# Decoder step on one core: a shared weight unit for the index columns, rotary by shuffles, array halves in turn, 25 tiles a chunk step

## What is computed

```python
def _rope(x, pos):                       # the first quarter of each head is rotated
    x1, x2 = x[..., :half], x[..., half:rot]
    return jnp.concatenate([x1 * cos - x2 * sin, x2 * cos + x1 * sin, x[..., rot:]], axis=-1)
...
    proj = h @ p['w_in']
    qa, ka, va, qi, ki, wi, ga, gb = _split_last(proj[..., :N_IN_A], COLS_A)
    qa = _rope(qa...); ka = _rope(ka...)            # 8 heads of 128
    qi = _rope(qi...); ki = _rope(ki...)            # 8 index queries and 1 index key of 64
    o_a = attn_fn(qa, ka, va, qi, ki, wi)           # index scores pick the keys to attend to
    pb = proj[..., N_IN_A:]                         # r, k, v, decay 64, a 64, gate 160 columns
    o_b, wkv = _rwkv7(pb, pb_prev, wkv0, p)         # delta-rule state, token by token
    mixed = sigmoid(ga) * (o_a @ w_pa) + sigmoid(gb) * (o_b @ w_pb)
    x = x + mixed @ p['w_o']
    # then RMSNorm, SwiGLU, residual
```

## Time and profile before

| | us |
|---|---|
| median of 3 runs (lowest, highest) | 2019.15 (2017.89, 2021.63) |
| the profiled execution: first to last instruction (span) | 2018.5 |
| TensorE matmul busy | 1977.0 (98%) |
| VectorE busy | 1059.1 (52%) |
| ScalarE busy | 731.0 (36%) |

### The profile page before, as it was taken

The page is one execution under the profiler, slowest core; times in us unless marked ns, Lnnn a source line. Parts: engine busy times, 40 slices in busy tenths (PEclk is TensorE's granted clock), DMA queues, the critical chain, the costliest instruction groups (busy, mean ns, idle before and its releaser), DMA issues.

```text
span 2018.5 us, 38203 instructions
## 1 busy us (share of the span) xinstructions
PE 1977.0 (98%) x15709; PEld 1796.7 (89%) x15709; DVE 1059.1 (52%) x1265; ACT 731.0 (36%) x964; POOL 44.4 (2%) x63
## 2 busy tenths in 40 slices
PE   8999999999999999999999999999999999999996
PEld 7999776678875776699999999999999999999996
DVE  6655976378873520254445554444444445444434
ACT  6333101532233110244444454444444444333332
POOL 0000002200000000000000000000000000000000
PEclk9999998999999999999999999999999999999998
DMA  6544257344558899844456554444444444654543
GB/s 266 178 153 163 105 193 184 95 135 139 171 198 293 286 387 385 316 147 165 166 180 211 190 175 163 164 165 163 165 164 164 166 165 153 206 170 159 170 158 117
DMA packets 103625, 378.15 MB, mean 187 GB/s; under 512 B 26994, under 2 KB 36850, under 8 KB 76146
## 3 DMA queue, kind: packets, MB, share of 16 engines
q1 hardware_dynamic: 78802, 346.88, 49.2%
q0 software_dynamic: 4736, 18.80, 2.9%
q10 hardware_dynamic: 20000, 11.28, 2.0%
HBM read 359.30 MB, written 17.58 MB: 187 GB/s over the span
## 4 chain that ended last, share of the span: by engine, by line
PE 93%; DVE 3%; DMA 1%; SPq 1%; ACT 1%; issue 1%; DVEq 0%; ACTq 0%
PE ps L467 17%; PE ps L1080 14%; PE ps L1081 14%; PE ps L1082 14%; PE ps L1035 5%; PE ps L1036 5%; PE ps L1037 5%; PE ps L500 2%; PE ps L499 2%; PE ps L501 2%; PE ps L942 1%; PE ps L991 1%; PE ps L511 1%; PE ps L663 1%; DVE arena L1703 1%; DMA ring<-in_wst 1%
## 5 line engine op out<-in xcount | busy, mean ns | idle before, releaser
L2006 DVE TENSOR_TENSOR weights_lo<-ring,weights_hi 128x2048 fp32r<-128x2048 f32 (+1 forms) x152 | 305.6, 2011 | 284.8 <-ACT weights_hi L1523 284.8
L1081 PE MATMUL ps<-h_lo,weights_hi 128*128 128x288 f32 x1408 | 416.1, 296 | 0.0
L1080 PE MATMUL ps<-h_hi,weights_hi 128*128 128x288 f32 x1408 | 414.6, 294 | 0.3 <-DVE weights_lo L2006 0.3
L1082 PE MATMUL ps<-h_hi,weights_lo 128*128 128x288 f32 x1408 | 412.5, 293 | 0.0
L1523 ACT ACTIVATE weights_hi<-ring 128x2048 fp32r<-128x2048 f32 (+1 forms) x152 | 257.1, 1691 | 365.7 <-PE ps L1082 356.7
L467 PE MATMUL ps<-hT,ring 128*128 128x288 f32 x1472 | 384.9, 414 | 0.0
L467 PEld LDWEIGHTS ps<-hT,ring 128*128 128x128 f32 x1472 | 274.4, 191 | 79.5 <-issue 8.0
L1082 PEld LDWEIGHTS ps<-h_hi,weights_lo 128*128 128x128 f32 x1408 | 265.1, 188 | 0.0
L1080 PEld LDWEIGHTS ps<-h_hi,weights_hi 128*128 128x128 f32 x1408 | 264.2, 188 | 0.5 <-DVE weights_lo L2006 0.5
L1081 PEld LDWEIGHTS ps<-h_lo,weights_hi 128*128 128x128 f32 x1408 | 264.4, 188 | 0.1
L1080 PE MATMUL ps<-act_hi,weights_hi 128*128 128x288 f32 x704 | 208.4, 296 | 0.0
(11 more groups left out here) (356 smaller groups left out, 2953.5 us busy)
## 6 DMA issues: line engine op xcount, KB each, us to landing
ring<-in_wst SPq DMA_DIRECT2D x209, 1024.0 KB, 4.9
ring<-in_wdn SPq DMA_DIRECT2D x64, 704.0 KB, 4.1
arena<-in_v SPq DMA_DIRECT2D x64, 512.0 KB, 5.8
arena<-in_kT SPq DMA_DIRECT2D x112, 256.0 KB, 5.6
arena<-chunk_ar_bk ACTq DMA_DIRECT2D x24, 256.0 KB, 4.0
arena<-in_ki SPq DMA_DIRECT2D x64, 64.0 KB, 2.1
arena<-in_kT SPq DMA_DIRECT2D x8, 512.0 KB, 6.5
arena<-in_xT SPq DMA_DIRECT2D x4, 592.0 KB, 7.0
```

The lines of the kernel that those rows point to most:

```text
L1080: mm(out, W_HI[:, (u - U_FF) % 2, w], hi, start=start, stop=False)
L1081: mm(out, W_HI[:, (u - U_FF) % 2, w], lo, start=False, stop=False)
L1082: return mm(out, W_LO[:, u % 4, w], hi, start=False, stop=stop)
L2006: tt(W_LO[:, u % 4, 0:m], raw, W_HI[:, at, 0:m].bitcast(F32), ALU.subtract).then_inc(sem("w_split"), 1)
```

## The change

- **Shared unit.** The index key (64 columns) and index weights (8, padded to 32) move into the unit of the last 32 gate columns. The two units they filled are gone: 6 index units become 4. VectorE copies the rows out after unit 2 (two copies and a shuffle, 1633 to 1635 of the new file), and ScalarE's tanh and sigmoid wait for that. The gate's second product takes 128 rows of `G2` instead of 32.
- **Rotary by shuffles.** VectorE's `stream_shuffle` swaps rows inside groups of 32 partitions and the sign is in the sine table. The index rotary is four operations over all five blocks at once, after the gram masks; a chunk step's rotary is four operations on 32 partitions and two heads. All permutation matmuls are gone.
- **Halves in turn.** The lora products and the state terms alternate between the two halves of the array.
- **Tiles moved.** Six index tiles stand between the lora groups, the others follow the norm sums; a chunk step fills 25 tiles (4, 6, 5, 4, 6). One store buffer moves.

```diff
-U_SMALL, U_RKV, U_IDX, U_VKQ, U_GA, ... = 0, 3, 27, 33, 57, ...
+U_SMALL, U_RKV, U_IDX, U_VKQ, U_GA, ... = 0, 3, 27, 31, 55, ...
             for j in range(2 * CT):
+                if j % 4 == 0 and j:
+                    fill(U_IDX, j // 2 - 2, j // 2)
                 if j >= 4:
                     pe.wait_ge(sem("lora_out"), j - 3)
-                at = 64 * (j // CT)
-                mm(..., LORA[at:at + 64, (j % CT) * P:(j % CT + 1) * P], SW[at:at + 64, :],
+                at = 64 * (j % 2)
+                mm(..., LORA[at:at + 64, (j // 2) * P:(j // 2 + 1) * P], SW[at:at + 64, :],
...
-            tiles(U_IDX, U_VKQ, h_tok, NT)
+            fill(U_IDX, 6, 4 * KT)
+            vkq(-32, 0)
...
-            for j in range(5):
-                if j >= 2:
-                    fill(U_VKQ, 61 + 2 * j, 63 + 2 * j)
-                    pe.wait_ge(sem("rope_idx_out"), j - 1)
-                mm(ps[5 + j % 2][:, 0:NT], c_("ropeI"), IDXT[:, j, :], ...)
-            fill(U_VKQ, 71, 75)
-            pe.wait_ge(sem("rope_idx_out"), 5)
+            vkq(65, 75)
...
-                for at in (0, 64):
-                    for b in range(NB):
+                for b in range(NB):
+                    for at in (0, 64):
                         ins = mm(first[at:at + 64, j, :, b, :], SST[at:at + 64, j, b, :],
...
-                fill(U_VKQ, at, at + 5)
+                fill(U_VKQ, at, at + 4)
...
-                if n:
-                    rotate(2 * n - 2)
-                    rotate(2 * n - 1)
-                fill(U_VKQ, at + 18, at + 22)
+                fill(U_VKQ, at + 15, at + 19)
...
+                if u == 2:
+                    dve.wait_ge(sem("mixed"), 3)
+                    cp(KI[0:64], SG[0:64, 1, :]).then_inc(sem("index_rows"), 1)
+                    nc.vector.stream_shuffle(KI[64:P], SG[0:64, 1, :], list(range(32))).then_inc(...)
+                    cp(WI[64:64 + IH], SG[64:64 + IH, 1, :]).then_inc(sem("index_rows"), 1)
...
-            for j in range(5):
-                dve.wait_ge(sem("rope_idx"), j + 1)
-                x = IDXT[:, j, :]
-                ch(tt(ROPI[:, 0, :], ps[5 + j % 2][:, 0:NT], c_("sinI"), ALU.mult))
-                ch(tt(ROPI[:, 1, :], x, c_("cosI"), ALU.mult))
-                tt(x, ROPI[:, 0, :], ROPI[:, 1, :], ALU.add).then_inc(sem("rope_idx_out"), 1)
+            ch(nc.vector.stream_shuffle(flat(ROPI), flat(IDXT), swap_idx))
+            ch(tt(ROPI, ROPI, c_("sinI")..., ALU.mult))
+            ch(tt(IDXT, IDXT, c_("cosI")..., ALU.mult))
+            tt(IDXT, IDXT, ROPI, ALU.add).then_inc(sem("rope_idx_out"), 1)
...
             def rotate(n):
-                dve.wait_ge(sem("rope"), n + 1)
-                ...
+                dve.wait_ge(sem("bank_free"), U_VKQ + 2 + HA + 2 * n + 2)
+                x, t, shape = KQ[0:32, 2 * n:2 * n + 2, :], ROPT[0:32], [32, 2, NT]
+                ch(nc.vector.stream_shuffle(flat(t), flat(x), swap_head))
+                ch(tt(t, t, c_("sinA")[0:32]..., ALU.mult))
+                ch(tt(x, x, c_("cosA")[0:32]..., ALU.mult))
+                tt(x, x, t, ALU.add).then_inc(sem("rope_out"), 1)
```

More of the change, by code:

```diff
@@ L88, in constants @@
         sin[:half] = sin[half:rot] = np.sin(ang)
[L89 to L93, removed]
+        sin[:half] *= -1.0
         put("cos" + name, np.tile(cos, (reps, 1)))
@@ L364, in _ @@
             ki_pages(0)
-            units(8, U_VKQ + 7, unit)
+            units(8, U_VKQ + 9, unit)
             for c in range(NCH):
@@ L369, in _ @@
             ki_pages(1)
-            units(U_VKQ + 7, U_VKQ + 9, unit)
+            units(U_VKQ + 9, U_VKQ + 11, unit)
             ki_pages(2)
@@ L391, in k_half @@
                         "a p n -> p (a n)")[:, w]).then_inc(sem(f"k_in{half}"), 16)
-            units(U_VKQ + 9, U_GA + 1, unit)
+            units(U_VKQ + 11, U_GA + 1, unit)
             sp.wait_ge(sem("wkvs_out"), 16)
@@ L843, in chunk @@
                 ins.then_inc(sem("chunk_done"), 1)
[L844 removed]
+                fill(U_VKQ, at + 19, min(at + 25, 3 * HA * KT))
             pe.wait_ge(sem("sample_act"), 63)
             for n in range(NCH):
[L848 to L851 removed]
+                chunk(n, at_tile + 25 * n)
             pe.wait_ge(sem("state"), NCH + 1)
@@ L865, in _ @@
             ins.then_inc(sem("vrows"), 1)
+            pe.wait_ge(sem("rope_out"), HA)
             def pscore(n):
@@ L913, in y_turn @@
                         mm(out, G2[:, 0, j * P:(j + 1) * P], SG[:, 0, :], start=True, stop=False)
-                        mm(out, G2[0:32, 1, j * P:(j + 1) * P], SG[0:32, 1, :], start=False, stop=True).then_inc(
+                        mm(out, G2[:, 1, j * P:(j + 1) * P], SG[:, 1, :], start=False, stop=True).then_inc(
                             sem("gate"), 1)
@@ L1203, in _ @@
             fn(BV, BV, ACT.Sqrt).then_inc(sem("act_stage"), 1)
-            for j in range(6):
+            for j in range(4):
                 u = U_IDX + j
                 act.wait_ge(sem("unit_read"), u + 1)
-                dst = QI[:, j, :] if j < 4 else (KI if j == 4 else WI)
-                fn(dst, ps[u % 2][:, 0:NT], ACT.Copy).then_inc(sem("bank_free"), 1)
+                fn(QI[:, j, :], ps[u % 2][:, 0:NT], ACT.Copy).then_inc(sem("bank_free"), 1)
             evicted = [0]
@@ L1408, in _ @@
             for n in range(NCH):
-                chunk(n, at_tile + 29 * n)
+                chunk(n, at_tile + 25 * n)
             act.wait_ge(sem("vrows"), 1)
@@ L1845, in _ @@
                 chunk(n)
-            for n in (2 * HA - 2, 2 * HA - 1):
-                rotate(n)
+            rotate(HA - 1)
             for name, n in (("sbk_in", 32), ("sti_in", 32), ("sar_in", 16), ("sgr_in", 16)):
```

135 lines of the change are left out of this document (63 added, 72 removed).

## The result

The changed kernel takes **2001.96 us** (2000.32 to 2002.86, 4 runs) against 2020.2 (2017.89 to 2021.63, 4 runs) before: ratio 0.9906, 95% interval 0.9893 to 0.9918. It is faster, as forecast, but by 18 us instead of 29, and outside the range of 1982 to 1997.

What follows compares the result with a forecast made beforehand. TensorE was taken as the bound (93% of the chain). Index part to pair 3's scores 5.1, chunk steps 22.3 and tail 1.5 sum to 28.9 us off 2018.5, 1989.6; plus 0.65 for the median, 1990 us, range 1982 to 1997.

Steps and rivals of the forecast that it cites:

- Chunk steps, 22.3 us: Chunk stage: a step falls from 23.54 to 20.6 us if VectorE follows; with two units' tiles removed, 22.3 us gained.
- Index keys, 5.1 us: Pair 3's scores: late key copies and lost clock leave 5.1 us of the earlier gains; bounds 0 and 7.6.
- Lora, norm, gram: Lora to gram products: groups of 1.17 us, norm sums after 8.2 (10.4 without overlap), gram products 0.5 us earlier.
- nothing; up to 1.4 us: Kernel start: VectorE's three added operations before ScalarE's tanh cost nothing, or up to 1.4 us without cover.
- Index rotary, 3 us earlier: Index part: VectorE's four operations take 6.6 us; line 727's products start near 315.9 instead of 318.42, less 0.5.
- State terms, 0.7 us each: State terms before the index scores: alternating halves save 0.7 us each, 5.6 for the eight, more if clock stays full.
- Tail, 1.5 us: After the last chunk: V transposes start earlier and key scores move up from 604.76 to 603.3, 1.5 us (0.5 to 2).
- The gate's longer load … nothing: After the first key scores: the gate's longer load is small beside the key pages; nothing, up to 1 us.
- VectorE as the bound: Rival: VectorE sets the chunk step; 2007 us with slow shuffles, 1994 at twice the plain rate; chance 0.15.
- Clock in the chunk steps: Rival: TensorE's clock falls in chunk steps, making the kernel slower, 2130 us if in all eight; chance 0.03.
- Keys without a clock cost: Rival: waits for index keys cost no clock and copies come sooner; first term 8 to 12, 1983 to 1986; chance 0.15.
- Halves that don't overlap: Rival: array halves don't overlap in lora and state terms; VectorE's chain 2.2 us late, 1992 us; chance 0.07.

Runs made afterwards that it cites:

- E2: Changed kernel, but TensorE's x products wait for the first four of ScalarE's eight turned copies, not all eight: 1995.79 us.
- E4: Changed kernel with pair 1's index-key copies issued earlier, before and among the gram stores: 1987.59 us.
- E6: Changed kernel with lora products and their read-outs in the old order, one array half and then the other: 2004.47 us.
- E1: The changed kernel run again, unaltered, as the point of reference: 1999.29 us.
- E15: Changed kernel, waiting for eight turned copies in chunk 0 and only four in the other seven chunks: 1996.35 us.
- E11: Changed kernel with the earlier index-key copies of E4 and the state terms in their old order, half by half: 2001.01 us.
- E7: Changed kernel with the second gate product on 32 rows of `G2` again instead of 128: 2004.06 us.
- E13: Changed kernel with E2's edit, and SP reading the second sequence's page numbers before its wait for the last chunk: 1990.15 us.
- E8: Changed kernel with every rotary shuffle of the chunk steps and the index part issued twice: 2002.32 us.
- E12: Every rotary shuffle issued twice, in the changed kernel with three repairs (E2's, E4's, page numbers read earlier; 1978.68 us): 1983.55 us.
- E14: Changed kernel, waiting for four turned copies in chunk 0 alone and eight in the other seven chunks: 1996.64 us.
- E9: Changed kernel with one weight tile of each chunk step moved back behind the turns (7 tiles there): 1997.54 us.

## Why the prediction was wrong

The direction held, and so did what was said of the removed work; the sum was too large by 10.7 us of span, most of it in the chunk steps. By landmarks of TensorE:

| up to | forecast gain | measured |
|---|---|---|
| pair 3's scores | 5.1 | 3.25 |
| first x products (two tiles less) | 6.1 | 3.4 |
| last x products | 25.5 | 16.25 |
| first key scores | 28.9 | 19.56 |
| end of span | 28.9 | 18.2 |

So 1.85 us are missing by pair 3's scores, 0.85 more by the first x products (0.57 of it chunk 0's wait for ScalarE), 6.55 more by the last, 0.1 in the tail and 1.35 behind it.

- **Chunk steps, 22.3 us: the step that failed.** "That only holds if VectorE follows": I looked at VectorE alone. ScalarE's turned copies need 3.2 us behind the turns, and the stretch that covers them went from 3.4 to 2.9 us. Before, the cover was used up to 0.3 us (488.25 and 488.54 above), and no row that I had chosen showed ScalarE there. Over the seven steps the gain is 12.85 us, not 19.4: 6 x 0.49 us of the wait, and 3.7 us in chunk 0 with its stop and low clock. With the wait taken away (E2) a step is 20.45, so the forecast of 20.6 was right for the tiles and products removed, to 0.15. The 20.5 us of work that I gave VectorE were too many: I took two waits off the old step and counted every other gap as work, 20.28, where the window of that step has it busy 19.60. In E2 it is busy 19.8.
- **Index keys, 5.1 us: mis-sized, 3.25 measured.** Keys were there at 344.88 (346.0 forecast), and the wait was 7.2, not 5. But the clock cost 6.0 us (E4 against the changed kernel), not 3. I took half of the six microseconds at half clock behind the gram wait of before (288.7 to 295.0); here it was low from the wait to beyond 355 us. The bounds of 0 and 7.6 held it.
- **Lora, norm, gram.** The group's 1.17 us came as forecast (starts 2.34 apart with its two tiles), with the norm sums 8.55 us after the lora start (8.2 forecast). The gram products start 0.9 us later instead of 0.5 earlier: from the lora start on, they stand where they stood (93.6 us behind it), so the 0.5 did not come. VectorE's first reciprocal starts 16.49 us behind the lora start where 14.91 stood, 1.6 later and not 1.2, and that used up the slack. The bound without overlap, 10.4, was too low: E6 has 12.0. The lora start is 0.95 later in this execution, and from 0.2 earlier to 1.0 later in E1 to E15, so "nothing; up to 1.4 us" for the start holds. By the ratios, E6 gives the taking of turns 2 to 5 us in all, not clear of the noise.
- **Index rotary, 3 us earlier:** measured 3.1, by luck. The gram products started 0.9 later instead of 0.5 earlier, and the four operations took 6.9 us, not 6.6. What made up for it was not in the forecast: a wait of 2.78 us of VectorE for a gram store is gone, so its masks end 0.9 us earlier. Before, then now:

```profile
306.70 0.69 DVE L1721 TENSOR_TENSOR arena<-ps,cst 128x512 f32<-128x512 f32 x1 [2.78 <-DMA gram<-arena]
```

```profile
307.52 1.82 DVE L1721 STREAM_SHUFFLE arena<-arena 128x1440 f32<-128x1440 f32 x1
```

- **State terms, 0.7 us each:** 1.10 for 1.82. Both halves write ps7, each to its own 64 partitions, so the trace again speaks against the Trainium skill (TensorEngine Tiling (Array Packing), Gotcha 1). That all of it is lost in a wait was forecast too, but not that with the keys in time it is worth more than its 5.8 us (E11), most of it clock by the one profile.
- **Tail, 1.5 us:** from the last x products to the key scores 18.87 us instead of 22.18, within 0.2 of the forecast.
- **Behind the tail, no term at all.** "The gate's longer load … nothing": I costed its load and not its product, which gained 3.1 us (E7), and the key pages, whose waits took 3.9 more (E13 against E2): 0.8 of the 1.1 us lost by 632 us.
- **The rivals.** VectorE as the bound: not here (E2, E8), but it is the next one, within 0.8 us (E12). Clock in the chunk steps: from chunk 1 on, windows of whole steps are at 1.00; chunk 0's is at 0.93, behind its stop. Keys without a clock cost: no (and by its own terms, 8 to 12 us, that rival would have given 1983 to 1987). Halves that don't overlap: they do. None of the rivals had ScalarE in it.

## What to carry to other kernels

When filler work is taken out of a stretch, list every engine that works under that stretch and how much of the cover each uses, not just the busiest one: here ScalarE, 36% busy, had 0.3 us of cover left, and VectorE, 52% busy, did not set the step. Price a wait of TensorE with the clock that it loses behind it, and try two edits together as well as alone: the order of the state terms was worth 0 or 13 us, according to when a transfer was issued. And a gain upstream must be followed through each transfer that starts at its end.

## What the runs showed of the hardware

- **Half clock without a wait.** With 32 instructions of 64 x 64 x 8 in 1.82 us between tiles, TensorE stood at 0.50 from 345 to 360 us while busy 5.00 of each 5.00 us (E11); with the same 32 alternating between array halves (1.10 us) it was at 1.00 (E4). The alternation is no guarantee: in E2 it fell to 0.50 from 325 to 337 us, again busy 5.00 of 5.00.
- **Rows that save nothing.** Products of 288 columns that alternate between 128 and 32 rows of contraction take 1.36 us a pair (E7); 128 and 128, 0.97. The 0.2 us at each change of shape is what the earlier trace rows had shown behind small products.
- **A shuffle costs little more than an arithmetic operation.** 32 x 576 take 0.79 us, with the mask load at 0.00, against 0.74; 128 x 1440 take 1.82 against 1.66.
- **A stop inside a run of 32 instructions** (1.0 to 1.8 us, always behind the 23rd of line 809), in nine kernels. It came with a wait of 0.56 us some six microseconds ahead (E15) and went without it (E14), but E9 has it with no wait. Its cause is open.
